# Spreading sixteen small TensorE products over four tiles and two PSUM banks, and their norm rows over one bank

## The reference, cut to what matters

```python
kk = (k * k_k).reshape(B, T, H, N)
kk = kk / jnp.maximum(jnp.sqrt(jnp.sum(kk * kk, -1, keepdims=True)), 1e-12)
...
# S_t = S_{t-1} diag(w_t) - (S_{t-1} kk_t) (a_t*kk_t)^T + v_t k_t^T ; y_t = S_t r_t
```

## Time and profile before

| What | Value |
|---|---|
| Median of 3 runs | 2252.8 us (2252.72 to 2254.31) |
| The profiled execution | 2255.68 us, of which the span of the core 2253.9 us |
| TensorE busy | 2166.9 us, 96% of the span |
| VectorE, ScalarE busy | 1487.3 us (66%), 1075.9 us (48%) |
| TensorE clock | full, but for short stretches; mean 0.985 |
| The stage that the change touches | 1268 to 1412 us |

### The profile page before, as it was taken

How to read it: one execution, slowest core, us unless ns; L and a number is a source line. 1 busy time by engine, 2 the same in 40 slices (tenths; PEclk the granted TensorE clock), 3 DMA queues, 4 the chain that set the end, 5 groups by cost and what they waited for, 6 DMA issues and landing times.

```text
span 2253.9 us, 40054 instructions
## 1 busy us (share of the span) xinstructions
PE 2166.9 (96%) x15548; PEld 1859.8 (83%) x15548; DVE 1487.3 (66%) x2038; ACT 1075.9 (48%) x1508; POOL 93.3 (4%) x77
## 2 busy tenths in 40 slices
PE   8999999999999999999899999997799999999997
PEld 6888878888888888888788878877687888888886
DVE  6656568885588856876873689863476544567655
ACT  5444554444444434445544655433334534456533
POOL 0800000000000000000000000002110000000000
PEclk9999999999999999999999999999999999999998
DMA  8654545555565555555365455643344555654552
GB/s 290 208 159 150 171 146 178 186 188 187 190 190 187 186 187 189 191 165 199 130 208 159 164 158 169 206 137 72 105 158 146 169 185 188 192 147 140 169 184 84
DMA packets 402744, 384.06 MB, mean 170 GB/s; under 512 B 43505, under 2 KB 401137, under 8 KB 401777
## 3 DMA queue, kind: packets, MB, share of 16 engines
q1 hardware_dynamic: 402610, 382.18, 53.3%
HBM read 374.78 MB, written 7.34 MB: 170 GB/s over the span
## 4 chain that ended last, share of the span: by engine, by line
PE 87%; DVE 8%; issue 2%; ACT 2%; DMA 0%; DVEq 0%; SPq 0%; ACTq 0%
PE acc L769 45%; PE acc L772 22%; PE acc L793 3%; PE aux L1121 3%; PE acc L848 2%; PE acc L849 2%; PE acc L850 2%; DVE w_lo L1964 2%; PE acc L796 2%; PE acc L1121 1%; PE aux L1277 1%; PE aux L1036 1%; PE aux L865 1%; ACT w_hi L1352 1%; PE aux L1056 1%
## 5 line engine op out<-in xcount | busy, mean ns | idle before, releaser
L1964 DVE TENSOR_TENSOR w_lo<-raw_w,w_hi 128x1024 fp32r<-128x1024 f32 (+1 forms) x592 | 713.9, 1226 | 455.5 <-ACT w_hi L1352 454.4
L1352 ACT ACTIVATE w_hi<-raw_w 128x1024 fp32r<-128x1024 f32 (+1 forms) x592 | 612.7, 1046 | 676.7 <-PE acc L772 575.2
L769 PE MATMUL acc<-h,w_hi 128*128 128x512 f32 x1664 | 525.9, 397 | 1.2 <-DVE w_lo L1964 1.2
L772 PEld LDWEIGHTS acc<-h,w_lo 128*128 128x128 f32 x1664 | 312.6, 188 | 73.8
L772 PE MATMUL acc<-h,w_lo 128*128 128x256 f32 x1664 | 327.0, 278 | 0.0
L769 PEld LDWEIGHTS acc<-h,w_hi 128*128 128x128 f32 x1664 | 254.6, 189 | 2.2 <-issue 1.4
L769 PE MATMUL acc<-x_split,w_hi 128*128 128x512 f32 x704 | 225.2, 401 | 0.0
L769 PE MATMUL acc<-ff,w_hi 128*128 128x512 f32 x704 | 221.7, 396 | 2.4 <-DVE ff L2220 2.4
L769 PE MATMUL acc<-xs_b,w_hi 128*128 128x512 f32 x512 | 162.5, 399 | 1.7 <-DVE w_lo L2408 0.9
L772 PEld LDWEIGHTS acc<-ff,w_lo 128*128 128x128 f32 x704 | 132.2, 188 | 31.2
L772 PEld LDWEIGHTS acc<-x_split,w_lo 128*128 128x128 f32 x704 | 132.2, 188 | 31.2
(11 more groups left out here) (366 smaller groups left out, 3146.3 us busy)
## 6 DMA issues: line engine op xcount, KB each, us to landing
raw_w<-in_w_up SPq DMA_DIRECT2D x176, 512.0 KB, 3.5
raw_w<-in_a_w_in SPq DMA_DIRECT2D x128, 512.0 KB, 3.3
raw_w<-in_w_in SPq DMA_DIRECT2D x64, 512.0 KB, 4.1
raw_w<-in_w_down SPq DMA_DIRECT2D x64, 512.0 KB, 3.3
raw_w<-in_b_w_qg SPq DMA_DIRECT2D x64, 512.0 KB, 3.8
raw_w<-in_w_o SPq DMA_DIRECT2D x32, 512.0 KB, 3.2
raw_w<-in_a_w_out SPq DMA_DIRECT2D x32, 512.0 KB, 3.3
raw_w<-in_w_k_shared SPq DMA_DIRECT2D x32, 512.0 KB, 3.3
```

Source lines behind the costliest of these rows:

```text
L769: pe.matmul(ACC[2 * b + f], WHI[:, q, k, f * P:(f + 1) * P], op[:, kt, :, :].rearrange("p h t -> p (h t)"), start=first, stop=False)
L772: mm = pe.matmul(ACC[2 * b + f][:, 0:T], WLO[:, slot, k, f * P:(f + 1) * P], op[:, kt, 0, :], start=False, stop=last)
L1352: act.activation(WHI[:, u % 4, 0:ku, :], RAWW[:, u, 0:ku, :], ACT.Copy).then_inc(hi_made, 1)
L1964: dve.tensor_tensor(WLO[:, u, 0:ku, :], RAWW[:, u, 0:ku, :], WHI[:, u % 4, 0:ku, :].bitcast(F32), ALU.subtract)\
```

## The change

The products for odd chunks (c = 1, 3) put each head's result into the other half of the partitions and into a second bank: `LT_BANKS` is `AUX[1]` and `AUX[2]`, columns 0 to 127. So the eight products of a tile f address all four tiles of 64x64 where before they addressed two. The copy reads two banks and puts the chunks back in order. `load_t` reads the swapped halves of the scratch for odd chunks. Since `AUX[2]` now holds products, all expansions go to `AUX[0]`, and expansion f waits for normalisation f - 1. (The helper `by_two` and all table positions stay.)

```diff
+        LT_BANKS = SIDE[:, 1:3, 0:P]
...
-                        sp.dma_start(TB[at:at + H, m, :, H * b:H * b + H], src[c, hh, b, :, 4 * g:4 * g + 4, :])\
+                        sp.dma_start(TB[at:at + H, m, :, H * b:H * b + H], src[c, hh ^ c % 2, b, :, 4 * g:4 * g + 4, :])\
...
-                    sp.dma_start(CRS[64 * hh:64 * hh + H, m, :, H:], cross[c, hh, 2, :, 4 * g:4 * g + 4, :]).then_inc(t_loaded[m], 16)
+                    sp.dma_start(CRS[64 * hh:64 * hh + H, m, :, H:], cross[c, hh ^ c % 2, 2, :, 4 * g:4 * g + 4, :]).then_inc(t_loaded[m], 16)
...
             def kk_expand(f):
-                if f >= 2:
-                    pe.wait_ge(kk_ready, f - 1)
-                expand_of_four(AUX[f % 2 * 2][:, 0:T], INVR, f).then_inc(kk_wide, 1)
+                if f >= 1:
+                    pe.wait_ge(kk_ready, f)
+                expand_of_four(AUX[0][:, 0:T], INVR, f).then_inc(kk_wide, 1)
...
             def lt_product(f):
-                        mm = pe.matmul(AUX[1][64 * h_:64 * h_ + 64, c * CHUNK:(c + 1) * CHUNK], part(BET, h_, f, c), part(KAP, h_, f, c),
-                                       start=(c == 0), stop=(c == NCH - 1))
+                        b, e, j = h_ ^ c % 2, c % 2, c // 2
+                        mm = pe.matmul(LT_BANKS[64 * b:64 * b + 64, e, j * CHUNK:(j + 1) * CHUNK], part(BET, h_, f, c), part(KAP, h_, f, c),
+                                       start=(j == 0), stop=(j == 1))
...
             def lt_out(f):
-                act.activation((XS, US)[p][:, :, :], by_chunk(AUX[1][:, 0:T]), ACT.Copy)\
+                act.activation((XS, US)[p][:, :, :].rearrange("p (j e) t -> p e j t", e=2), by_two(LT_BANKS), ACT.Copy)\
...
             def kk_normal(f):
-                dve.scalar_tensor_tensor(KAP[:, f, :], K[:, f, :], PV[:, c:c + 1], AUX[f % 2 * 2][:, 0:T], ALU.mult, ALU.mult)                   .then_inc(kk_ready, 1)
+                dve.scalar_tensor_tensor(KAP[:, f, :], K[:, f, :], PV[:, c:c + 1], AUX[0][:, 0:T], ALU.mult, ALU.mult)                   .then_inc(kk_ready, 1)
```

## The result

The changed kernel takes 2271.38 us (median of 4 runs, 2268.27 to 2274.76), against 2252.76 us: ratio 1.0084, 95% interval 1.0065 to 1.0103, which is 19 us slower (15 to 23). The forecast was 13.1 us slower, 2265.9 us, with a range up to 2271. The median lies 0.4 us above that range. Direction and place were right; some 6 us were missing.

A forecast was written before the change was run, and what follows sets the result against it. TensorE, busy for 96% of the span, was taken to bound the kernel. Waits of 16.9 us less 3.8 us saved on products gave 13.1 us more, 2252.8 + 13.1 = 2265.9 us, range 2259 to 2271 us.

The forecast's parts named there:

- Part 1: 16 products on four tiles: each 0.235 us shorter, saving 3.8 us in all (bounds: nothing and 4.3 us).
- Part 2: Copy out of two banks and stores with swapped halves: cost nothing.
- Part 3: All expansions in one bank: nine wait on TensorE for normalisation f - 1, at full size, costing 16.9 us.
- One bound: Upper bound on the cost of the expansions' waits: 18 us, if the shorter product counts against the other eight too.
- the clock: Rival: TensorE falls to half clock behind new pauses, 10 us at half clock, 5 us lost, 2271 us; chance 0.05.
- Healing: Rival: VectorE catches up after first stalls; stalls under 3.8 us (chance 0.06) or half healed, 2257.4 us (0.06).
- tiles that don't overlap: Rival: the products between full-size matmuls gain nothing from four tiles, 2269.7 us; chance 0.03.

The follow-up runs named there:

- the waits alone: Against the kernel before, only the single bank for all expansions and the wait for normalisation f - 1, products on two tiles and one bank as before: 2276.15 us, ratio 1.0103.
- the second trace: The kernel before run once more with no edit: 2253.35 us, ratio 0.999.
- the second trace of the changed kernel: The changed kernel run once more with no edit: 2276.47 us, ratio 1.0094 against the kernel before.

## Why the prediction was right, and where it failed

**Part 1, products: right.** 0.22 us each instead of 0.235, 3.5 us instead of 3.8. The row from the recurrence, 15 ns per instruction, was the better guide than the Trainium skill's floor of about 25 ns in "TensorE: Matmul & The Clock Gate", section "Wait — 56ns, not 53.3ns?": 16 instructions now lie within a merged row of 0.46 us, of which 0.22 us is the last one's own duration. What remains is 0.24 us from the first start to the last, where that floor asks for 0.375. The section gives the floor for matmuls however small and doesn't speak of tiles.

**Part 2, copy and stores: right.** The copy takes 384 to 385 ns from two banks against 385 from one, and no wait for a store appeared.

**Part 3, the waits: right, all nine, with their sizes.** Forecast 16.9 us, measured 17.1, none at f = 1 to 4, 8 and 12. That they come at full size each time and don't heal rests on the anchor: ScalarE waits for the product that stands one unit ahead of the expansion, and both the normalisation and the expansion count from it. The 0.2 us of expansion 9 are shown by the waits alone. One bound was added up wrongly: if the shorter product counted against the other eight waits too, that would be 16.9 + 1.9 = 18.8 us, not 18. It bears on nothing, since with four tiles the other eight waits are the same as with two, to 0.03 us.

**The step that failed: the clock, which the sum left out.** The sum has no term for it. It stood among the rivals, at a chance of 0.05, on the ground that the longest new pause (2.9 us) was hardly above one of 2.81 us in the recurrence that had left the clock alone. That took one harmless pause for a bound. Even in the kernel before, the pause at that place wasn't always harmless: in the second trace it was 3.36 us long, and the clock was at 0.50 for 6.8 us around its end:

```profile
1595.12 0.38 PE L1121 MATMUL aux<-wkv_small 64*64 64x64 f32 x3 [3.36 <-issue]
...
1593.80:1600.60 6.80, 5.48 (x136) 5.48 (x137) 1.93 (x5) 1.04 (x3) 0.61 (x1) 0.50 0.19 45
```

And in the stage pauses half as long lower the clock: behind the 1.5 us of expansion 5 in the second trace of the changed kernel, behind those of 2.0 us of expansions 7 and 10 in both. And the same pause does it in one execution and not in another. At the end of the feed-forward layer, far ahead of the change, TensorE pauses in the kernel before and in the changed kernel's second trace alike:

```profile
1005.12 0.73 PE L769 MATMUL acc<-ff,w_hi 128*128 128x512 f32 x2 [1.83 <-DVE ff L2220]
...
1005.50:1008.70 3.20, 3.20 (x20) 2.80 (x19) 2.48 (x4) 1.83 (x3) 0.00 (x0) 1.00 0.06 20
```

```profile
1005.91 1.09 PE L770 MATMUL acc<-ff,w_hi 128*128 128x512 f32 x2 [1.84 <-DVE ff L2222]
...
1006.20:1009.40 3.20, 3.20 (x11) 2.62 (x11) 2.32 (x3) 1.06 (x2) 0.00 (x0) 0.50 0.11 39
```

1.83 us with the clock at 1.00 behind it, 1.84 us with 0.50; in the other seven traces of all kernels the clock stays at 1.00 there. So one trace couldn't say that such pauses are safe. What the runs show in place of the missing term: of nine new pauses of 1.2 to 2.9 us in a stage that had none, four, six and five lowered the clock in the three traces, for 6.2, 9.3 and 7.6 us. The smallest of these on top of 13.1 us gives 19.3 us and 2272 us. The size that the rival gave it was nearly right: it allowed for three stretches, 10 us at half clock and 5 us lost, where the first trace has four, 13.6 us and 6.2. What was wrong was its chance of 0.05, and with it the sum. That the result lies only just above the range is owed to this rival, whose 2271 us set the upper end.

**Healing** didn't take place; **tiles that don't overlap** neither.

## What to carry to other kernels

A wait on an engine that was never idle has two prices, its length and what it does to TensorE's clock, and the second came to between a third and just over half of the first here (6.2 and 9.3 us on 17.1). Count it for each new pause of the lengths that showed it here, 1.5 us and more, and don't take a pause that did nothing in one trace as safe. When one buffer has to serve where two did, read off for each use how late its last reader is: those differences were the stalls to within 0.1 us in eight of nine cases, and 0.3 us too small in the ninth, where the change itself had shortened TensorE's way to the wait. Where the reader is late by about one step of the schedule (2.9 us at most here, against 2.8 us for a unit), try moving the writer by a step, which here turned 19 us lost into 5 us won.

## What the hardware showed that was not expected

- Of the seven pauses of 1.5 to 2.9 us in otherwise dense work, four were followed by 3.4 us at 1.2 GHz in one execution, six in another and five in the kernel with the waits alone, the pauses being at the same places and of the same lengths but for expansion 9's. The two pauses of 1.2 us (expansions 11 and 14) never were, in three traces. What decides in between was not settled.
- Filling the pauses with useless matmuls kept the clock at 1.00 in the stage, which was 6.2 and 9.3 us shorter than in the two traces of the changed kernel.
- Putting two kinds of small matmuls next to each other instead of between full-size ones saved some 0.2 us each time.
